# A four-layer hybrid backbone: three adaLN groups multiplied on VectorE during the input projections, and one group moved from a routing stage to the mLSTM heads

## The reference

```python
def ada_mod(cvec, w, b):
    m = jax.nn.silu(cvec) @ w + b            # (1024,) @ (1024, 6144)
    return m.reshape(cvec.shape[0], 6, D_MODEL)

def modulate(h, shift, scale):
    return h * (1.0 + scale[:, None, :]) + shift[:, None, :]

for i in range(4):                           # mixer: 0 pooling, 1 mLSTM, 2 latent attention, 3 pooling
    mod = ada_mod(c, w_ada[i], b_ada[i])
    h = modulate(rmsnorm(x, norm_mix[i]), mod[:, 0], mod[:, 1])
    x = x + mod[:, None, 2] * mixer_i(h)
    h = modulate(rmsnorm(x, norm_ffn[i]), mod[:, 3], mod[:, 4])
    x = x + mod[:, None, 5] * moe(h, ...)    # 16 experts, top 2 of a group
```

## Time and profile before

| | |
|---|---|
| median of three runs | 1325.13 us (1319.93 to 1325.91) |
| profiled execution | 1324.39 us, span 1322.7 us |
| TensorE busy | 1200.5 us, 91% |
| VectorE, ScalarE busy | 383.4 us (29%), 316.7 us (24%) |
| mean rate of the DMA engines | 295 GB/s |
| TensorE's share of the chain that ended last | 76% |

### The profile page before, as it was taken

How to read it: one execution, slowest core, us unless ns; L and a number is a source line. 1 busy time by engine, 2 the same in 40 slices (tenths; PEclk the granted TensorE clock), 3 DMA queues, 4 the chain that set the end, 5 groups by cost and what they waited for, 6 DMA issues and landing times.

```text
span 1322.7 us, 24788 instructions
## 1 busy us (share of the span) xinstructions
PE 1200.5 (91%) x10404; PEld 697.5 (53%) x10404; DVE 383.4 (29%) x1218; ACT 316.7 (24%) x716; POOL 122.6 (9%) x188
## 2 busy tenths in 40 slices
PE   4788998789998899899978999999999997789996
PEld 2446544447885554654447643445465444565544
DVE  1345111340004522621132023341451115561113
ACT  1240111231124522211133211230411114401113
POOL 2000100210000000111020000000002111001101
PEclk9898999889999999899989999999999998989998
DMA  9999999794326873898979223891689987658993
GB/s 349 412 421 421 409 413 421 282 350 151 119 96 247 298 314 140 321 409 347 412 271 351 69 96 106 357 363 64 251 344 357 419 359 277 273 214 355 397 390 136
DMA packets 89708, 389.57 MB, mean 295 GB/s; under 512 B 10456, under 2 KB 38604, under 8 KB 53240
## 3 DMA queue, kind: packets, MB, share of 16 engines
q1 hardware_dynamic: 71568, 336.61, 65.2%
q0 software_dynamic: 17456, 51.07, 10.5%
q10 hardware_dynamic: 568, 0.23, 0.1%
HBM read 370.96 MB, written 27.96 MB: 302 GB/s over the span
## 4 chain that ended last, share of the span: by engine, by line
PE 76%; DMA 10%; DVE 5%; SPq 3%; issue 3%; ACT 2%; POOL 1%; POOLq 0%; DVEq 0%; ACTq 0%
PE bank L491 70%; DMA sb_ring<-in_w_ada 3%; PE bank L966 3%; SPq L449 2%; DMA slot_out<-sb_arena,sb_homes 2%; DMA sb_arena<-slot_out,sb_slots 2%; DMA sb_ring<-in_w_exp_up 2%; POOL sb_arena L2132 1%; DVE sb_xT L1994 1%; PE bank L984 1%; DMA slot_out<-sb_arena 1%; DMA sb_arena<-token_rows,sb_rows 1%; PE bank L894 0%; DVE sb_arena L1954 0%; PE bank L1017 0%
## 5 line engine op out<-in xcount | busy, mean ns | idle before, releaser
L491 PE MATMUL bank<-sb_ring,sb_arena 128*32 128x256 f32 (+1 forms) x6112 | 449.9, 429 | 17.3 <-DMA sb_ring<-in_w_exp_down 8.0
L491 PEld LDWEIGHTS bank<-sb_ring,sb_arena 128*32 128x32 f32 x6112 | 212.5, 111 | 197.8 <-issue 108.0
L491 PE MATMUL bank<-sb_arena 128*128 128x128 f32 (+11 forms) x776 | 140.7, 361 | 10.9 <-DVE sb_arena L1840 7.0
L491 PE MATMUL bank<-sb_ring,sb_hT 128*128 128x256 f32 x624 | 140.8, 387 | 6.2 <-ACT sb_hT L1225 6.2
L491 PEld LDWEIGHTS bank<-sb_ring,sb_hT 128*128 128x128 f32 x624 | 120.6, 194 | 26.9 <-issue 9.1
L491 PEld LDWEIGHTS bank<-sb_arena 128*128 128x128 f32 (+2 forms) x776 | 102.7, 194 | 45.6 <-issue 13.0
L491 PE MATMUL bank<-sb_ring,sb_cond 128*2 128x512 f32 x768 | 94.9, 616 | 8.8 <-DMA sb_ring<-in_w_ada 8.5
L491 PE MATMUL bank<-sb_arena,sb_ring 128*128 128x384 f32 (+2 forms) x288 | 95.5, 507 | 3.0 <-DVE sb_arena L1710 2.1
L1941 DVE TENSOR_TENSOR sb_arena<-sb_arena,bank 128x256 f32<-128x256 f32 x40 | 16.8, 421 | 248.9 <-PE bank L491 248.9
L491 PE MATMUL bank<-sb_hT,sb_ring 128*128 128x384 f32 x256 | 85.8, 498 | 2.6 <-ACT sb_hT L1225 2.6
L491 PEld LDWEIGHTS bank<-sb_arena,sb_ring 128*128 128x128 f32 (+1 forms) x288 | 49.9, 181 | 44.9 <-issue 19.0
(11 more groups left out here) (318 smaller groups left out, 1013.8 us busy)
## 6 DMA issues: line engine op xcount, KB each, us to landing
sb_ring<-in_w_ada SPq DMA_DIRECT2D x96, 1024.0 KB, 8.7
sb_ring<-in_w_exp_gate SPq DMA_DIRECT2D x60, 1024.0 KB, 10.4
sb_ring<-in_w_exp_up SPq DMA_DIRECT2D x60, 1024.0 KB, 12.7
sb_ring<-in_w_exp_down SPq DMA_DIRECT2D x60, 1024.0 KB, 15.1
sb_ring<-in_w_mlstm_in SPq DMA_DIRECT2D x12, 1024.0 KB, 12.1
token_rows<-sb_arena POOLq DMA_DIRECT2D x12, 512.0 KB, 7.6
slot_out<-sb_arena POOLq DMA_DIRECT2D x9, 512.0 KB, 8.8
sb_scratch<-in_w_exp_gate SPq DMA_DIRECT2D x4, 1024.0 KB, 9.0
```

Source lines behind the costliest of these rows:

```text
L491: return pe.matmul(out, lhsT, rhs, start=first, stop=last)
```

## The change

Groups 4, 8 and 9 are no longer multiplied by TensorE. VectorE adds up, in two rows of 2048 columns per partition (one per conditioning vector, in free space of `scratch`, `hT` and `arena`), weight times conditioning value over the eight units (`mix`); ScalarE makes the first product of one of the two rows (`mixed_first`). The sum over the 128 partitions is then eight matmuls with a column of ones (`ada_sum`). Group 4 is done in the mLSTM projections, 8 and 9 in the attention projections; their units are interleaved with the projections' weights and skipped by `take`. The heads of the mLSTM have groups 5, 6 and 7, so layer 1's routing has none. The attention has group 10 alone, one unit in every second step from 4 to 18, and its transposes in step 21; the transposes of group 9 are in step 1. In `mla`, VectorE's copy of the first position part comes before the rotation of the keys. Semaphores are renamed (`turns_full`, `gate_tok`), and ScalarE's squares go to `vt_early`, since `knT` now holds sums. The diff, cut to its core:

```diff
+        in_squares = [[(scratch[:, 0:2048], 0, 2048)], [(scratch[:, 2048:3072], 0, 1024), (view(13512, 1024), 1024, 2048)]]
+        in_keys = [[(view(5568, 2048), 0, 2048)], [(view(7616, 2048), 0, 2048)]]
+        in_latents = [[(hflat[:, 0:2048], 0, 2048)], [(hflat[:, 2048:3072], 0, 1024), (view(0, 1024), 1024, 2048)]]
+        ACC = {4: in_squares, 8: in_keys, 9: in_latents}
+        MIXED = tuple(ACC)
+        BESIDE = {c: (10, (c - 4) // 2) for c in range(4, 20, 2)}
+        COLUMNS_BESIDE = {21: 10}
...
+        def mixed_units(g, *rows):
+            for k in rows:
+                mixed_unit[g, k] = len(units)
+                add((A["w_ada"][g // 3, k * P:(k + 1) * P, (g % 3) * UNIT:(g % 3 + 1) * UNIT], 1, UNIT), UNIT,
+                    (acc_mixed, mixed_done[g, max(k, 1)]))
...
-        ADA_MIXER = [(), (4, 5, 6), (8, 9, 10), ()]
-        ADA_WINDOW = [(3,), (7,), (11,), ()]
+        ADA_MIXER = [(), (5, 6, 7), (10,), ()]
+        ADA_WINDOW = [(3,), (), (11,), ()]
...
                 for i in range(4):
                     add((w[:, i * 256:(i + 1) * 256], KC, 256), 2048, (qk_full, 2 * (i + 1)))
+                    if i:
+                        mixed_units(4, *((0, 1), (2, 3), (4, 5))[i - 1])
                 for i in range(4):
                     add((w[:, 1024 + i * 256:1024 + (i + 1) * 256], KC, 256), 2048, (v_full, NT * (i + 1)))
+                    if i == 0:
+                        mixed_units(4, 6, 7)
...
                 for i in range(3):
                     add((w[:, i * 256:(i + 1) * 256], KC, 256), 2048, (pl_full, NT * (i + 1)))
+                    mixed_units(8, *((0, 1), (2, 3, 4), (5, 6, 7))[i])
                 for i in range(4):
                     add((A["w_mla_qb"][j][:, i * 384:(i + 1) * 384], QL // P, 384), 1536, (qp_full, i + 1))
+                    mixed_units(9, 2 * i, 2 * i + 1)
...
+            def ada_sum(g):
+                pe.wait_ge(mrow_ready, g)
+                pe.wait_ge(mod_added, g)
+                pe.wait_ge(acc_mixed, mixed_done[g, KC - 1])
+                for c in range(2):
+                    for q in range(4):
+                        ap, a = [(ap, a) for ap, a, b in ACC[g][c] if a <= q * 512 < b][0]
+                        ins = mm(ps[7][32 * q:32 * q + 2, :], order[:, 4 - c:6 - c], ap[:, q * 512 - a:(q + 1) * 512 - a],
+                                 c == 0, c == 1)
+                ins.then_inc(ada_unit, KC)
...
+                ada_sum(4)
...
+                        if c == 4:
+                            ada_columns(4)
...
                     if i == 1:
                         rotate(0, kpT[:, KEYS - LAT:KEYS])
+                        ada_sum(8)
+                ada_columns(8)
...
                 pe.wait_ge(rope_ready, 5)
+                ada_sum(9)
...
-                    ada_beside(ADA_MIXER[2], c)
+                    if c == 1:
+                        ada_columns(9)
+                    ada_beside(c)
...
+            def mixed_first(g):
+                i = MIXED.index(g)
+                arrived(act, mixed_unit[g, 0])
+                for ap, a, b in ACC[g][0]:
+                    ins = act.activation(ap, slot(mixed_unit[g, 0])[:, a:b], ACT.Copy, scale=cond[:, 0, 0:1])
+                ins.then_inc(acc_set, 1)
...
+            def mix(g, *rows):
+                i = MIXED.index(g)
+                for k in rows:
+                    w = slot(mixed_unit[g, k])
+                    arrived(v, mixed_unit[g, k])
+                    for c in (1, 0):
+                        if c == 0 and k == 0:
+                            continue
+                        if c == 0 and k == 1:
+                            v.wait_ge(acc_set, i + 1)
+                        if c == 1 and k:
+                            v.wait_ge(acc_mixed, mixed_done[g, k - 1] - (len(ACC[g][0]) if k > 1 else 0))
+                        if c == 0 and k > 1:
+                            v.wait_ge(acc_mixed, mixed_done[g, k - 1])
+                        for ap, a, b in ACC[g][c]:
+                            if k:
+                                ins = v.scalar_tensor_tensor(out=ap, in0=w[:, a:b], scalar=cond[:, k, c:c + 1], in1=ap,
+                                                             op0=ALU.mult, op1=ALU.add)
+                            else:
+                                ins = v.tensor_scalar(ap, w[:, a:b], cond[:, k, c:c + 1], None, ALU.mult)
+                            ins.then_inc(acc_mixed, 1)
...
+                mix(4, *range(KC))
+                v.wait_ge(turns_full, 2)
...
+                mix(8, 0, 1, 2, 3, 4)
                 v.wait_ge(prs_ready, 1)
...
+                mix(8, 5, 6)
                 v.wait_ge(prs_ready, 2)
...
+                mix(8, 7)
                 v.wait_ge(kp_full, 1)
...
-                rope(0, kpT[:, KEYS - LAT:KEYS])
-                for i in range(4):
+                v.wait_ge(pl_full, 12)
+                def positions(i):
                     v.wait_ge(qp_full, i + 1)
                     v.tensor_copy(qpT[:, i, :], ps[(3 * i + 2) % 4][:, 0:TOK]).then_inc(qp_raw, 1)
+                mix(9, 0, 1)
+                positions(0)
+                mix(9, 2, 3)
+                rope(0, kpT[:, KEYS - LAT:KEYS])
+                positions(1)
+                mix(9, 4)
+                positions(2)
+                mix(9, 5)
+                positions(3)
...
+                mod_columns(8)
                 for c in range(8):
+                    if c == 4:
+                        mix(9, 6, 7)
                     v.wait_ge(vt_full, c + 1)
```

More of the change, by code:

```diff
@@ L302, in build @@
         NCONST, NMLA = 8, 12
+        in_squares = [[(scratch[:, 0:2048], 0, 2048)], [(scratch[:, 2048:3072], 0, 1024), (view(13512, 1024), 1024, 2048)]]
[5 more added lines that the diff above has]
+        COLUMNS_BESIDE = {21: 10}
+        mixed_unit = {}
+        mixed_done = {}
+        n_mixed = 0
+        for g in MIXED:
+            for k in range(KC):
+                n_mixed += len(ACC[g][1]) + (len(ACC[g][0]) if k else 0)
+                mixed_done[g, k] = n_mixed
         units = []
@@ L493, in _ @@
             state = {"u": 0}
+            by_vector = set(mixed_unit.values())
             def take():
                 u = state["u"]
+                while u in by_vector:
+                    u += 1
                 state["u"] = u + 1
@@ L518, in ada_columns, with ada_beside @@
                 ins.then_inc(ada_full, 1)
[L520 to L527 removed]
+            def ada_beside(c):
+                if c in BESIDE:
+                    ada(*BESIDE[c])
+                if c in COLUMNS_BESIDE:
+                    ada_columns(COLUMNS_BESIDE[c])
             def norm(n):
@@ L1190, in mod_rows @@
                 act.activation(mrow[:, :], ps[7][:, :], ACT.Copy).then_inc(mrow_ready, 1)
-            def rows_beside(groups, step):
-                i, at = step // 7, step % 7
-                if i < len(groups) and at == 4:
-                    mod_rows(groups[i])
+            def mixed_first(g):
[4 more added lines that the diff above has]
+                ins.then_inc(acc_set, 1)
             def norm_scale(n):
@@ L1512, in mod_columns @@
                 settle()
-            def columns_beside(groups, step):
-                i, at = step // 7, step % 7
-                if i < len(groups) and at == 5:
-                    mod_columns(groups[i])
+            def mix(g, *rows):
[19 more added lines that the diff above has]
+                            ins.then_inc(acc_mixed, 1)
             def norm(n, gain):
```

54 lines of the change are left out of this document (29 added, 25 removed).

## The result

The changed kernel took 1317.68 us, the median of 20 runs, against 1324.47 for the kernel before in runs taken beside them: a ratio of 0.9943, with a 95% interval of 0.9929 to 0.9956, so 6 to 9 us less. The forecast was 1311.5 and the range held the time, but the gain is about half of the 13.5 us that the sum gave. The time lies just under 1318.5, the prediction's bound for "faster", and outside the 1305 to 1317 that it gave to its forecast proper. The profiled execution is one of the longer ones, 1321.33 us with a span of 1319.6.

What follows compares the result with a forecast made beforehand. TensorE was taken as the bound in every stage touched. Terms of +2.3, -1.65, +2.1 and -16.2 us sum to -13.5, taking 1324.39 to 1310.9 (1311.6 against the median); predicted 1311.5, range 1304.5 to 1320.

Steps and rivals of the forecast that it cites:

- rival 1: Attention: with fewer fillers the softmax chain sets the pace; 1319 if half the saved 14.8 us turns idle; chance 0.12.
- the second rival: Attention: TensorE's clock falls with fewer fillers, costing up to 32.7 us more, 1344 us; chance 0.04.
- VectorE's price: One multiply-add over 2048 columns on VectorE: 2.36 us whole, 2.57 in two pieces.
- its idle time before the turned rows: Layer 1's mLSTM projections: VectorE still has 32 us of cover before the copy due at about 360.
- the missing wait near 762: Attention projections: TensorE's 2.10 us stall on the position copies goes, as the first copy comes earlier.
- wrong if under 0.9: Attention: the prediction calls itself wrong if the granted clock there falls under 0.9.
- mLSTM projections, +2.3: Layer 1: group 4's sum on TensorE, 1.83 us, and its four transposes, 0.5, add 2.3 us.
- Heads, 0: Layer 1's mLSTM heads: still three groups, 5, 6, 7 in place of 4, 5, 6, so no change.
- Layer 1's routing, -1.65: Group 7 leaves: 1.25 us from logits to experts, read off layer 3, and 0.4 for transposes; bounds 0 to -1.65.
- Attention projections, +2.1: Layer 2: sums of groups 8 and 9 at 1.83 us each, transposes 0.5, less the 2.1 us stall.
- Attention, -16.2: Layer 2: eight single units replace twelve pairs, -14.8 us; a 0.99 stall and 0.5 of transposes also go.
- the row of 882 to 890: Late attention without units: TensorE busy 8.00 of 8 us at full clock, taken as evidence against rivals 1 and 2.

Runs made afterwards that it cites:

- the kernel with fewer fillers: Full change, but group 7 stays in layer 1's routing and the mLSTM heads have only groups 5 and 6; ratio 0.9965 to before, -4.5 us.
- the turns ahead: Full change with only group 9's transposes moved ahead of the attention's first step; ratio 0.9895 to before.
- the busy routing: Full change plus matmuls nobody reads in TensorE's idle stretches in the routing of layers 1 and 3; ratio 0.9879 to before, 14.8 us less.
- the moved fillers: Full change with group 9's transposes ahead of the attention, group 10's units spread to its end, its transposes behind the output projection; ratio 0.9879 to before.
- layer 1's part: Kernel before with only group 4 mixed on VectorE and group 7 in the mLSTM heads, attention layer unchanged; +1.3 us against before.
- the attention's part: Kernel before with only groups 8 and 9 mixed on VectorE, position copy first, group 10 as filler, layer 1 unchanged; -8.1 us against before.

## Why the prediction was right, and where it was not

The direction, the class and the range held; the time lay 6 us above the forecast. That was in part luck: 1317.68 lies in the band (1316 to 1325) that the prediction gave to rival 1, whose mechanism the traces refute, and what took the time is the second rival in small, to which it gave 0.04. Of its signs, VectorE's price, its idle time before the turned rows and the missing wait near 762 came as said; the attention was 68.5 us and not near 64, layer 1's logits to experts 21.4 and not 20.0, and the attention's granted clock, "wrong if under 0.9", was 0.95 and 0.90. Step by step:

- **VectorE's price**: 2.36 and 2.57 forecast, 2.34 and 2 x 1.28 = 2.56 measured. The cover before the copy of the turned rows: 32 us forecast, 34.2 left.
- **mLSTM projections, +2.3**: over the same matmuls up to the heads 123.83 us against 121.44 (281.83 to 403.27) before, +2.4. **Heads, 0**: 74.31 and 74.31. Both right; a price of zero there may have hidden a benefit, since the kernel with fewer fillers gained 3 us less (intervals just overlapping).
- **Layer 1's routing, -1.65**: measured -0.25 (40.44 to 40.19). I named this edit's lower bound 0 for "half-clock phases", and that is what happened; the step that failed is reading the gain off layer 3 without asking what three new idle stretches of TensorE do to it. Layer 3's 20.03 us was not the bare chain either: filled, layer 1's same stretch took 18.4. With all three filled the stage took 38.00, -2.4.
- **Attention projections, +2.1**: measured +0.3. The 2.10 us stall was counted, and not the spell of 3.4 us behind it, worth 1.9. The same mechanism, in my favour, and luck: two other traces with the same stall have no spell there.
- **Attention, -16.2**: measured -13.2 in one trace of after (81.66 to 68.47) and -10.0 in the other (71.70). At full clock it is 64.81 with the turns ahead, against 80.03: -15.2, of which 0.6 is what the turns fill. The forecast for full clock, its -16.2 with the first pair's half clock (3.07 us against 1.90) taken off, was -15.0, so the term was nearly right for a TensorE at full clock: single units cost 0.97 and not 0.90 us each, and the last heads hold a little more idle time. The step that failed is the sentence that the clock's phase "will fall on other matmuls": it fell on the same stage and was 6.8 or 13.7 us long in all six traces, where before's attention has 3.4 or none, since the units behind the first wait were gone. This is the second rival, small: I looked for it in every turn of the heads, by the row of 882 to 890, and it came once, at the start.
- **Everything else, 0**: the routing of layers 2 and 3 is 4.3 us longer in the profiled execution with unchanged code, at a lower clock. The sum had no term for it. The tail behind layer 3's experts gave back another 3.5 us (from 1272.88 to the end of the span, 49.8 us, in before; from 1266.29, 53.3, in after): the store that the chain shows there took 9.95 us and not 8.32, the gather behind it 6.60 and not 5.95, also with code that is the same. These 2.3 us are DMA and not the clock. The store took 8.3 to 8.7 us in the three traces with before's code and 9.95 in both of the full change, but 8.7 to 10.5 in its variants; no run here isolates why. The routing and the tail are the largest misses of the sum.

In the runs, 0.006 of granted clock lies between the full change (0.9547, and 0.9541 over its 20 first runs) and before (0.9607). At 0.87 us for 0.001 this is 5.2 us, and -7.9 becomes -13.1 against a forecast of -13.5. The sum was about right for the work and had no account of the clock. Two experiments act on the clock and hardly on the sum (the turns ahead fill 0.6 us of a wait), and both got the missing time back: the busy routing (-14.8) and the turns ahead (-14.4). Both ran on the chip on which the full change did not; the pair on one chip is the moved fillers, 8 us under the full change, 2.6 of it from the spread units.

The Trainium skill, "TensorE: Matmul & The Clock Gate", section on HAM oscillation, prices throttled time at that time x (1 - 1.2/2.4). A mean clock lower by 0.001 over 1320 us is 2.64 us more at the lower level, so it would cost 1.32 us. The runs give 0.87. They differ, and the measurement decides; my guess, which no run here isolates, is that part of a spell passes while TensorE waits for another engine, where its clock costs nothing.

What stays open: why layer 3's routing has a spell of 13.7 us in its first stretch in both traces of the full change and in those of layer 1's part, the attention's part and the turns ahead, and 6.8 in before, in the moved fillers and with group 7 in routing. The code of the stage is the same in all of these. What lies ahead of the stage, or only the moment at which it starts, may decide, and these runs don't tell which. Also open are the 3 us of the busy routing's gain that its two stages don't show, and why the same wait in the same code is followed by a spell of one length in one execution and of another, or of none, in the next.

## What to carry to other kernels

In this kernel, work taken off a bound TensorE was worth its full time only where what was left still kept TensorE at full clock; before moving fillers away, look at what stands right behind each of its waits, and leave something there. Put real work that is due anyway (here four transposes) into the one wait that opens a stage before adding work for nothing. And compare the mean granted clock of the runs before the stages: a difference of a few thousandths can be as large as the effect in question.

## What the runs showed of the hardware that I had not expected

- The same wait of 1.43 us of TensorE was followed by no spell or 3.4 us at the lower clock where pairs of units came behind it (four traces), and by 6.8 or 13.7 us where they did not (six traces); 0.84 us there was followed by none, in all three traces that have the turns in it without matmuls of no use beside them in that place.
- A stall of 2.10 us in the middle of dense matmuls of 128x384 was followed by 3.4 us at the lower clock in one trace and by none in two.
- TensorE matmuls of no use made the kernel faster: ratio to before 0.9879 against 0.9940 (on two chips).
- Within one kernel on one chip the executions spread over 4 to 15 us, and the granted clock goes with much of it (correlation -0.79 over 162 executions).
